# An attention layer reordered: output products of three head pairs kept for the last turn, rotation ahead of the norm, o by tokens

## What is computed

```python
def odd_layer(x, positions, layer_idx, norm_w, w_in, q_norm_w, k_norm_w,
              lq1, lk1, lq2, lk2, subln_w, w_out):
    hn = rmsnorm_2(x, norm_w)
    proj = hn @ w_in                                  # 1024 -> 4096
    q, k, v, gate = jnp.split(proj, 4, axis=-1)
    q = rmsnorm_2(q.reshape(bsz, s, 8, 2, 64), q_norm_w)
    k = rmsnorm_2(k.reshape(bsz, s, 8, 2, 64), k_norm_w)
    q, k = partial_rotary(q, positions), partial_rotary(k, positions)
    lam = exp(sum(lq1 * lk1)) - exp(sum(lq2 * lk2)) + lam_init
    # per head: softmax of two score maps, block-causal in chunks of 64
    wts = pr[:, :, 0] - lam * pr[:, :, 1]
    o = wts @ v                                       # 8 heads x 128
    o = rmsnorm_2(o, subln_w) * (1.0 - lam_init)
    o = o.reshape(bsz, s, 1024) * jax.nn.silu(gate)
    return x + o @ w_out
```

## Time and profile before

| | |
|---|---|
| median of three runs | 2773.03 us |
| profiled execution | 2769.58 us, of which the span is 2767.8 us |
| TensorE busy in the span | 2618.2 us (95%) |
| odd layer, first input product to first transpose of the store | 2366.8 to 2754.6 us of the span |
| mean granted TensorE clock | 0.976 of 2.4 GHz |

### The profile page before, as it was taken

How to read it: one execution, slowest core, us unless ns; L and a number is a source line. 1 busy time by engine, 2 the same in 40 slices (tenths; PEclk the granted TensorE clock), 3 DMA queues, 4 the chain that set the end, 5 groups by cost and what they waited for, 6 DMA issues and landing times.

```text
span 2767.8 us, 32858 instructions
## 1 busy us (share of the span) xinstructions
PE 2618.2 (95%) x11934; PEld 2034.3 (74%) x11934; DVE 1596.1 (58%) x2703; ACT 1048.8 (38%) x1559; POOL 1140.0 (41%) x1446
## 2 busy tenths in 40 slices
PE   8999988999999888999999899998999988989996
PEld 6888777888887666777777688886887756756664
DVE  4644665777777523434334554556888953366565
ACT  3222343343343333323333422224436663445543
POOL 4666532333333343333333366664554424414320
PEclk9999999999999999999999999999999999999997
DMA  3333311112121221222222133322332212302110
GB/s 122 99 104 95 105 54 39 61 61 62 61 61 46 67 63 55 70 64 69 70 70 62 58 103 99 99 84 78 99 92 63 64 49 69 91 23 69 61 39 31
DMA packets 57106, 196.02 MB, mean 71 GB/s; under 512 B 6416, under 2 KB 8976, under 8 KB 56976
## 3 DMA queue, kind: packets, MB, share of 16 engines
q1 hardware_dynamic: 55824, 192.90, 22.4%
q10 hardware_dynamic: 1152, 1.38, 0.2%
HBM read 192.16 MB, written 2.10 MB: 70 GB/s over the span
## 4 chain that ended last, share of the span: by engine, by line
PE 85%; DVE 9%; ACT 3%; issue 2%; DMA 1%; SPq 0%; ACTq 0%; DVEq 0%
PE psum L310 23%; PE psum L312 22%; PE psum L311 22%; PE psum L1742 3%; PE psum L2426 1%; PE psum L2396 1%; DVE psum L884 1%; PE psum L423 1%; PE psum L2399 1%; PE psum L1748 1%; PE psum L2739 1%; PE psum L2420 1%; PE psum L1130 1%; PE psum L2768 1%; ACT whi L276 1%
## 5 line engine op out<-in xcount | busy, mean ns | idle before, releaser
L291 POOL TENSOR_TENSOR wlo<-raw,whi 128x256 fp32r<-128x256 f32 x1436 | 1139.5, 825 | 1565.5 <-ACT whi L276 1565.1
L310 PE MATMUL psum<-xh,whi 128*128 128x512 f32 x1832 | 764.4, 417 | 14.6 <-DVE xl L404 7.9
L312 PE MATMUL psum<-xh,wlo 128*128 128x512 f32 x1832 | 719.8, 393 | 0.0
L311 PE MATMUL psum<-xl,whi 128*128 128x512 f32 x1832 | 719.4, 393 | 0.0
L276 ACT ACTIVATE whi<-raw 128x1024 fp32r<-128x1024 f32 (+1 forms) x367 | 377.8, 1036 | 805.6 <-PE psum L312 805.6
L310 PEld LDWEIGHTS psum<-xh,whi 128*128 128x128 f32 x1832 | 347.5, 190 | 96.5 <-issue 29.0
L312 PEld LDWEIGHTS psum<-xh,wlo 128*128 128x128 f32 x1832 | 346.6, 189 | 75.9
L311 PEld LDWEIGHTS psum<-xl,whi 128*128 128x128 f32 x1832 | 347.7, 190 | 73.2 <-issue 9.8
L482 DVE TENSOR_TENSOR xT<-psum,xT 128x512 f32<-128x512 f32 x248 | 167.3, 688 | 207.7 <-PE psum L312 207.7
L310 PE MATMUL psum<-pool_yh,whi 128*128 128x512 f32 x256 | 102.5, 400 | 0.0
L311 PE MATMUL psum<-pool_yl,whi 128*128 128x512 f32 x256 | 101.7, 397 | 0.0
(11 more groups left out here) (533 smaller groups left out, 4515.6 us busy)
## 6 DMA issues: line engine op xcount, KB each, us to landing
raw<-weights_dram SPq DMA_DIRECT2D x335, 512.0 KB, 3.5
raw<-weights_dram SPq DMA_DIRECT2D x32, 384.0 KB, 3.0
xin<-x_dram SPq DMA_DIRECT2D x4, 512.0 KB, 6.9
out_dram<-y SPq DMA_DIRECT2D x4, 512.0 KB, 2.6
g_masks<-gdn_masks_dram ACTq DMA_DIRECT2D x1, 384.0 KB, 3.8
par<-params_dram SPq DMA_DIRECT2D x1, 326.5 KB, 3.0
mwork<-positions_dram ACTq DMA_DIRECT2D x1, 256.0 KB, 2.9
o_pT<-positions_dram ACTq DMA_DIRECT2D x1, 256.0 KB, 3.0
```

The costliest lines, as they stand in the source:

```text
L291: last = pool.tensor_tensor(wlo[:, q, part], raw[:, q, part], whi[:, q, part].bitcast(F32), ALU.subtract)
L310: pe.matmul(gbank(b), whi[:, q, c:c + P], h, start=k == 0, stop=False)
L311: pe.matmul(gbank(b), whi[:, q, c:c + P], l, start=False, stop=False)
L312: done = pe.matmul(gbank(b), wlo[:, q, c:c + P], h, start=False, stop=k == nk - 1)
```

## The change

The odd layer is written anew; the other layers stay.

- One unrolled section of 40 slots takes the place of a first, a looped and a last section. The tiles of a pair come in the order K, Q, V, the gates of a pair come in its own turn instead of the turn before, and the output slots of all four pairs stand last.
- Output products: `yh` and `yl` are kept for all four pairs. The 24 output tiles of pairs 0 to 2 are issued in turn 3, one per piece, between the steps where the other turns have input pieces. Only pair 3's eight tiles come after them.
- Preparation: the rotation product takes the raw K and Q with a matrix that has the gain in it (`turned`), and the cosine factor is applied to the raw values too. K is multiplied by 1/rms at the end (`kn`). Q is not normalized at all: sums of its squares are made by tokens (eight products with two output columns, `q_sums`), and 1/rms goes in as scale of the exponential (`srq`) and in its bias (`nsrq`). All of this stands between pieces of the turn before. For pair 0 it stands between the input tiles.
- Attention: V is transposed after the scores instead of ahead of them. `o` is made by tokens (stationary `pT`, moving `vt`, ten products of 128 columns for a head), ScalarE copies it and makes the sums of squares with `accum_out` (four activations of 128 columns), one Ln and one Exp serve both heads, VectorE scales (`scale_o`), and TensorE transposes back (`o_transposes`).
- The mask value is -1e30 instead of -3e37, since it now stands in unscaled scores.

The core of the diff:

```diff
+            def k_sum(pe, i, x):
+                pe.wait_ge(*ae.of(f"{i} square {x}"))
+                if i:
+                    pe.wait_ge(*(ae.of(f"{i} ln 0") if x else ve.of(f"{i - 1} v 1")))
+                else:
+                    pe.wait_ge(*ab.at("exp"))
+                pe.matmul(prep_bank(i, f"sum {x}"), halves, rr[:, x, :], start=True, stop=True)\
...
+            def turn_product(pe, i, x):
+                if i:
+                    pe.wait_ge(*(ve.of(f"{i} sin {x - 1}") if x else ae.of(f"{i} ln q")))
...
+            def pieces(pe, i):
+                for j in range(turn_at(i), turn_at(i) + (8 if i < PAIRS - 1 else 2)):
+                    for k in range(0, KD, 2):
+                        product(pe, S, 0, j, 0, xh, xl, None, k, k + 2)
                         yield
+                if i == PAIRS - 1:
+                    for h in range(PAIRS - 1):
+                        for m in range(KD):
+                            out_product(pe, h, m)
+                            yield
...
+                p_transposes(0, (0, 1))
+                v_transposes()
+                more(1)
+                p_transposes(0, (2, 3))
+                if not last_turn:
+                    k_sum(pe, i + 1, 0)
+                more(1)
+                o_products(0)
+                if not last_turn:
+                    k_sum(pe, i + 1, 1)
+                more(1)
+                p_transposes(1, (0, 1))
+                if not last_turn:
+                    q_sums(pe, i + 1)
+                more(1)
+                p_transposes(1, (2, 3))
+                if not last_turn:
+                    turn_product(pe, i + 1, 0)
+                more(2)
+                o_products(1)
+                for x in range(1, 4):
+                    if not last_turn:
+                        turn_product(pe, i + 1, x)
+                    more(2)
+                if last_turn:
+                    more(1)
+                for hd in range(2):
+                    o_transposes(hd)
+                    if last_turn:
+                        more(1)
+                for _ in rest:
+                    pass
...
+                    act.activation(dst, wbank(x % 4)[:, 0:w], ACT.Exp, scale=srq[:, x:x + 1], bias=nmx[:, x:x + 1],
+                                   accum_out=rs[:, x:x + 1]).then_inc(*ae.done(f"{i} exp {x}"))
```

More of the change, by code:

```diff
@@ L35 @@
 NEG = -3.0e37
+NEG_RAW = -1.0e30
 ROUND = 1.5 * 2.0 ** 23
@@ new lines, in q_sums @@
+            def q_sums(pe, i):
+                pe.wait_ge(*ae.of(f"{i} square 3"))
+                pe.wait_ge(*(ae.of(f"{i} ln 1") if i else ab.at("exp")))
+                for y in range(2 * NCH):
+                    hd, t = y // NCH, y % NCH
+                    last = pe.matmul(prep_bank(i, "sums q")[:, 2 * y:2 * y + 2], rr[:, 2 + hd, t * P:(t + 1) * P],
+                                     halves[:, 0:P:64], start=True, stop=True)
+                last.then_inc(*te.done(f"{i} sums q"))
@@ L2722, in work_tensor @@
-            def work_tensor(pe, i, more):
-                te.turn()
-                pe.wait_ge(*vp.at("rope 3", i))
-                for cc in range(NCH):
-                    for d in range(2):
-                        at = (cc % 2) * 2 * P + d * P
-                        last = pe.transpose(wbank(cc // 2)[:, at:at + P], vT[:, d, cc * P:(cc + 1) * P], ident)
-                last.then_inc(*te.done("v tokens"))
+                if i == PAIRS - 1:
[3 more added lines that the diff above has]
+                            yield
@@ L2776, in work_scalar @@
-            def work_scalar(act, i, after):
-                ae.turn()
+                          .then_inc(*te.done(f"{i} scores {x}"))
+                    more(2)
[9 more added lines that the diff above has]
+                    k_sum(pe, i + 1, 1)
@@ L2809, in normalize, with silu_gates, work_vector, fill @@
+            def silu_gates(act, i):
+                for d in range(2):
+                    act.wait_ge(*free(gate_at(i, d)))
+                    act.activation(gs[:, d, :], gs[:, d, :], ACT.Silu).then_inc(*ae.done(f"{i} silu {d}"))
+            def work_vector(dve, i):
+                last_turn = i == PAIRS - 1
+                taking = takes(dve, i)
+                def fill(n):
+                    for _ in range(n):
+                        next(taking)
                 def normalize(x):
@@ L2869, in tensor @@
+                scale_o()
+                if last_turn:
+                    fill(3)
+                for hd in range(2):
+                    gate_o(hd)
+                for hd in range(2):
+                    split_y(hd)
+                for _ in taking:
+                    pass
             def tensor(pe):
-                nv["first product"](pe, first_sec, 0, 0)
-                product(pe, first_sec, 0, 1, 0, xh, xl)
+                nv["first product"](pe, S, 0, 0)
+                product(pe, S, 0, 1, 0, xh, xl)
@@ L2925, in vector @@
-                loop(dve, PAIRS - 1, turn)
-                work_vector(dve, PAIRS - 1, lambda t: None)
-                for j in (0, 1):
-                    add_to_x(dve, last_sec, 0, j, range(4 * j, 4 * j + 4))
+                take(dve, 2, xq[:, 2, :])
+                lam_vector(dve)
+                cos(dve, 0, 0)
+                take(dve, 3, xq[:, 3, :])
+                cos(dve, 0, 1)
+                sin(dve, 0, 0)
+                for x in range(2, 4):
+                    cos(dve, 0, x)
```

580 lines of the change are left out of this document (346 added, 234 removed).

## The result

The changed kernel takes 2729.32 us (median of four runs, 2726.28 to 2731.84) against 2772.84 for the kernel before; the ratio is 0.985, with a 95% interval of 0.9837 to 0.9862. The profiled execution took 2728.77 us, with a span of 2726.9. It is 43.5 us faster; 2736.5 was predicted, with a range of 2722 to 2757.

The account below looks back on a forecast made before the run. TensorE, busy 95% of the span, was taken as the bound. First scores 2415, three turns of 75 and turn 3's 78 give 2718 at the store; with the 13.2 us store 2733, plus 3.45 to the median: 2736.5 us, range 2722 to 2757.

Parts of the forecast that it names:

- Start of the layer: Odd layer up to pair 0's first scores: these come at 2415 us instead of 2442.3.
- the wait for lambda: At the layer's start, TensorE waits 2.7 us at the first sum for lambda's exponential, in place of 3.48.
- The half clock behind the wait: At the layer's start, a stretch at 1.2 GHz after lambda's wait, kept from the old kernel at some 1.4 us.
- Eight small sums for Q: In the preparation, eight two-column products, 16 records priced like transposes at 0.11 each: 1.8 us.
- A full turn: Score to score: 69.3 us of work and 5.1 of new waits, running sum 74.9, taken as 75 us.
- Turn 3: Last turn, first score to store: 78 us, with 65.8 before pair 3's eight tiles (11.3) and last addition (0.9).
- The cover: In turn 3, VectorE's 25.7 us stay below TensorE's 31, so filler hides them; waits of 2.5 us stay.
- VectorE's order: Rival, chance 0.20: in the turns, three late takes ahead of TensorE's needs cost 2 us more each; turn 81, total 2754.5.
- a stretch at half clock: Rival, chance 0.10: 3.4 us at 1.2 GHz in each full turn, or slower ScalarE, adds 5 to 11: about 2745.
- The waits did not vanish: Rival, chance 0.08: 15 of 15.3 us of waits in the turns and 2.7 at the start go: 2719.
- Banks never held up a kept tile: Rival, chance 0.05: in turn 3, 24 kept tiles each wait 2 us for banks VectorE frees; slower, 2785.
- its first rival: Chance 0.20: VectorE's takes ahead of sin and scaling hold TensorE longer; turns of 81 us, total 2754.5.

Follow-up runs that it names:

- experiment 2: Only pair 2's output products kept for turn 3, against the changed kernel: among the scores 2744.57 us; behind them, with gate pieces spread over eight score groups, 2735.67 us.
- experiment 4: The run gpsimd_quiet, against the changed kernel: ScalarE's slot copies, which set off GpSimd's splits, moved behind the tables; 2723.83 us.
- gpsimd_quiet: Changed kernel with ScalarE's slot copies at the start moved behind the tables, so GpSimd has nothing to do while VectorE makes the angle; 2723.83 us.
- start_block: Changed kernel with pair 0's preparation as one block behind all six input tiles, ahead of the first scores, instead of between the tiles; 2732.00 us.

## Why the prediction was right, and where its terms were off

- **Start of the layer**: 2415 predicted, 2419.95 measured. Of the 4.95 us, 0.5 lie ahead of the layer. The step that failed is the wait for lambda, 6.14 for 2.7: VectorE's 5.4 and 0.4 us came from rows beside a GpSimd that was idle for all but the first 0.8 us, and in the new order it works beside them. VectorE needs 9.3 us there, and 5.3 with GpSimd quiet. The half clock behind the wait cost 2.8 to 3.1 for 1.4. The rest was right: 19.6 of work and 1 for VectorE, against 20.94 of unbroken work.
- **Eight small sums for Q**: 16 records in 1.84 us, where 1.8 was taken from the transposes' row.
- **A full turn**: 75 predicted, 72.90 measured. Work 68.8 for 69.3. Waits 0.30, 0.96, 1.38 and 1.47, for 0.7, 1.2, 1.4 and 1.4; the 0.4 for the last exponential did not come, and the running sum of 74.9, rounded to 75, lay above 69.3 + 5.1. All causes were the named ones, the last of them with ScalarE close behind.
- **Turn 3**: 78 predicted, 75.15 measured. The cover held. Waits are 0.95 and 0.98, and 0.78 before the store, 2.7 in all for 3.4. Off is the work: TensorE's busy time is 72.4 where 63.3 + 11.3 = 74.6 was summed. Some 0.6 of that is the price of the 192 output matmuls (42 in a row take 9.72 us, 0.231 each, for 0.234); how the rest divides among transposes, `o` and the 18 changes between kinds was not separated.
- **Sum**: +4.95 at the start, -6.3 in the turns, -2.85 in turn 3: the store begins at 2713.8 instead of 2718. Errors of opposite sign hide each other: the start is off by 4.95 where the terms were called good to 2, a turn by 2.1 where it was 1.5, turn 3 by 2.85 where it was 3. That the time lies within 2728 to 2745 is in part luck. A further 2.9 us is the distance of the profiled execution to the median, 0.6 in the changed kernel, where 3.45 was carried over.
- **The reason for the gain** was given as 23 us of time in turn 3 that had nothing to do or ran at 1.2 GHz. Undoing the products' move alone costs 22.8 us (21.8 by the stretches). That it is the place behind the scores which pays most, experiment 2 shows, and the prediction did not say.
- **The rivals.** VectorE's order cost nothing beyond what was predicted; no turn had a stretch at half clock. The waits did not vanish. Banks never held up a kept tile in the changed kernel. In favour of its first rival the prediction counted three waits of 4 to 5 us in the old preparation; the earlier trace rows has two, 4.26 and 5.21.

How much of the gain is due to `o` by tokens and to Q's norm in the exponential was not separated; the trace shows their prices (20 records of `o` in 2.2 us, 0.09 us more for an exponential of any width with a scale by partition), and the turns with their own products, 83.95 for 84.3 to 86.0, bound what they bring together with the preparation's new place.

## To carry to other kernels

Work that can wait belongs into the stretch where the bound engine stands still, and there into the largest gap: eight tiles were worth 12.3 us behind the scores and 5.5 among them, and behind them they also brought the clock back. When two engines in order feed a third, look at what is late next before moving one instruction: the take alone was worth 1.5 us a turn, with ScalarE's squares 2.4. And read an operation's duration at a place where its neighbours are as busy as they will be.

## What the runs showed of the hardware

- VectorE slows beside GpSimd by the operand: 128x512 with two SBUF operands 1.11 instead of 0.69, a scalar operation on one SBUF operand 0.83 to 0.85 instead of 0.43 to 0.49, two of 128x128 1.47 instead of 0.47; with a PSUM operand no change. Moving GpSimd's work away gave them all back (experiment 4). GpSimd slows beside VectorE as well, 1.17 instead of 0.74 for 128x256.
- The length of a wait does not decide by itself whether half clock follows. One of 6.14 us was followed by a stretch at 0.50 that cost 2.8 us, one of 2.10 by none (a clock of 1.00 in gpsimd_quiet), but one of 1.90 in start_block, with the sixteen records of two columns behind it, by a stretch at 0.50. One of 2.85 ahead of the same sixteen cost 1.9 us (45.32 busy for 43.42):

```profile
2367.60:2415.77 48.17, 45.32 (x183) 33.27 (x181) 26.59 (x41) 26.10 (x35) 21.95 (x29) 0.96 0.32 97
```

- A turn in which nothing changes repeats to 0.06 us, within a run and between programs (72.90 to 72.96), while the layer's start wanders by 5 us. Stretches between landmarks resolve what the median of the whole does not.
